# The output projection of an encoder layer on one core: x fetched in spaced pieces, evictions reordered, turned tiles spread

## The reference

```python
y = jax.nn.sigmoid(m_a) * ya + jax.nn.sigmoid(m_b) * yb
x = x + y @ w_out[i]
g = jax.nn.sigmoid(_rms(x, ple_norm[i]) @ w_ple_gate[i])
x = x + (p[i] @ w_ple[i]) * g
```

## Time and profile before

| | |
|---|---|
| median of 3 runs | 1808.4 us (1806.47 to 1808.62) |
| the profiled execution's own time | 1807.8 us |
| its span, from the first to the last instruction | 1806.1 us |
| TensorE busy | 1767.6 us, 98% of the span |
| VectorE busy | 1282.9 us, 71% |
| ScalarE busy | 865.1 us, 48% |
| DMA, mean over the span | 131 GB/s |

### The profile page before, as it was taken

The page is one execution under the profiler, slowest core; times in us unless marked ns, Lnnn a source line. Parts: engine busy times, 40 slices in busy tenths (PEclk is TensorE's granted clock), DMA queues, the critical chain, the costliest instruction groups (busy, mean ns, idle before and its releaser), DMA issues.

```text
span 1806.1 us, 23828 instructions
## 1 busy us (share of the span) xinstructions
PE 1767.6 (98%) x9241; PEld 1517.4 (84%) x9241; DVE 1282.9 (71%) x1546; ACT 865.1 (48%) x1169; POOL 196.9 (11%) x203
## 2 busy tenths in 40 slices
PE   6999999999999999999999999999999989899998
PEld 5899999888888888888888888888888768788887
DVE  6977777777687878787887878784555688864333
ACT  7444444434375757474747565654222434434221
POOL 4000000000040404040303131310000000000000
PEclk9999999999999999999999999999999999999999
DMA  7344444575723332333332333344555466432332
GB/s 225 90 140 118 116 138 144 195 253 176 201 82 110 87 108 81 109 86 111 87 109 83 103 88 106 92 134 134 164 148 154 141 234 216 145 129 92 118 117 82
DMA packets 289286, 236.81 MB, mean 131 GB/s; under 512 B 9994, under 2 KB 234281, under 8 KB 288673
## 3 DMA queue, kind: packets, MB, share of 16 engines
q1 hardware_dynamic: 286128, 225.49, 41.6%
q0 software_dynamic: 3056, 9.96, 1.7%
HBM read 215.00 MB, written 20.41 MB: 130 GB/s over the span
## 4 chain that ended last, share of the span: by engine, by line
PE 90%; DVE 5%; issue 2%; DMA 2%; ACT 1%; SPq 0%; DVEq 0%; ACTq 0%
PE mm_ps L2037 13%; PE mm_ps L2039 13%; PE mm_ps L2038 13%; PE ax_ps L2024 2%; PE ax_ps L2026 2%; PE ax_ps L2025 2%; PE ax_ps L2038 2%; PE ax_ps L2037 2%; PE ax_ps L2039 2%; PE mm_ps L2263 2%; PE mm_ps L2262 2%; PE mm_ps L2261 2%; PE mm_ps L2026 2%; PE mm_ps L2024 2%; PE mm_ps L2025 2%
## 5 line engine op out<-in xcount | busy, mean ns | idle before, releaser
L364 DVE TENSOR_TENSOR w_lo<-w_raw,w_hi 128x1024 fp32r<-128x1024 f32 x188 | 236.0, 1257 | 251.7 <-ACT w_hi L355 251.6
L2037 PE MATMUL mm_ps<-act_hl,w_hi 128*128 128x512 f32 x960 | 383.1, 399 | 0.0
L355 ACT ACTIVATE w_hi<-w_raw 128x1024 fp32r<-128x1024 f32 x188 | 198.5, 1056 | 375.7 <-PE mm_ps L2039 157.5
L2039 PE MATMUL mm_ps<-act_hl,w_lo 128*128 128x512 f32 x960 | 375.0, 391 | 0.0
L2038 PE MATMUL mm_ps<-act_hl,w_hi 128*128 128x512 f32 x960 | 374.6, 390 | 0.0
L2039 PEld LDWEIGHTS mm_ps<-act_hl,w_lo 128*128 128x128 f32 x960 | 180.2, 188 | 38.7
L2038 PEld LDWEIGHTS mm_ps<-act_hl,w_hi 128*128 128x128 f32 x960 | 180.5, 188 | 36.1
L2037 PEld LDWEIGHTS mm_ps<-act_hl,w_hi 128*128 128x128 f32 x960 | 180.5, 188 | 36.0
L1046 ACT ACTIVATE q_hi<-q_raw 128x1024 fp32r<-128x1024 f32 x84 | 87.6, 1057 | 141.7 <-DVE q_raw L1408 81.3
L1399 DVE TENSOR_TENSOR q_lo<-q_raw,q_hi 128x1024 fp32r<-128x1024 f32 x84 | 101.8, 1224 | 52.6 <-ACT q_hi L1046 52.1
L921 POOL TENSOR_TENSOR key<-key,low_h 128x512 f32<-128x512 f32 x16 | 16.8, 1052 | 804.6 <-ACT key L1153 804.6
(11 more groups left out here) (372 smaller groups left out, 4194.8 us busy)
## 6 DMA issues: line engine op xcount, KB each, us to landing
w_raw<-in_w_in SPq DMA_DIRECT2D x120, 512.0 KB, 3.8
q_raw<-in_w_in SPq DMA_DIRECT2D x56, 512.0 KB, 5.9
r_in<-in_w_in SPq DMA_DIRECT2D x56, 512.0 KB, 4.6
w_raw<-in_w_out SPq DMA_DIRECT2D x36, 512.0 KB, 4.8
w_raw<-in_w_ple_gate SPq DMA_DIRECT2D x32, 512.0 KB, 3.8
...
```

The source lines that it names most:

```text
L355: nc.scalar.activation(w_hi[:, s, :], w_raw[:, r, :], ACT.Copy).then_inc(hi_done, 1)
L364: nc.vector.tensor_tensor(w_lo[:, s, :], w_raw[:, r, :], w_hi[:, s, :].bitcast(F32), ALU.subtract).then_inc(lo_done, 1)
L2037: MM(bank, wh, m_hi[:, k0 + k, :], start=start and k == 0, stop=False)
L2039: mm = MM(bank, wl, m_hi[:, k0 + k, :], start=False, stop=stop and k == kn - 1)
```

## The change

- The column `norm_c` is no longer fetched by SP at step 9 of group 0, but by POOL, far ahead, right after its last work on the heads.
- The four pieces of x for a group are no longer issued at one go. In group 0 piece t waits in addition for TensorE to be done with step 3 + 2t, in group 1 with step 2t, the first of these behind eviction 2 of group 0 (before: eviction 2 too, which then stood at step 16 of group 0).
- Evictions get an order for each group (`O_ORDER`) and new places (`O_AT`, `O_AFTER`): in group 0 eviction 1 goes from step 14 to 22, 4 to 7 from 18, 22, 24, 26 to 23 to 26, and evictions 2, 3 and 8 follow 9 and 10 into steps 1 to 5 of group 1. In group 1 the places stay. `ev(g, n, t)` turns an eviction into the count that a wait needs.
- The `sy_lo` of group 0 go from steps 4, 6, 9, 12 to 5, 7, 11, 15, and the last `y_lo` from step 4 to 6.
- The six turned tiles go from after steps 17 to 22 of group 1 to after steps 17, 18, 21, 22, 25, 26; tile 5's low part goes behind the first `w_lo` of the gate projection. `token_squares` goes from steps 4 to 11 to steps 8 to 15.

The diff, without most of its unchanged lines:

```diff
@@ -482,6 +482,15 @@
         SY_AT = {2: 1, 3: 2, 6: 3, 5: 4}
+        O_ORDER = ((0, 1, 4, 5, 6, 7, 2, 3, 8, 9, 10), tuple(range(11)))
+        O_AT = ({14: 0, 22: 1, 23: 4, 24: 5, 25: 6, 26: 7}, {13: 0, 14: 1, 16: 2, 17: 3, 18: 4, 22: 5, 24: 6, 26: 7, 27: 8})
+        O_AFTER = {1: 2, 2: 3, 3: 8, 4: 9, 5: 10}
+        TURN_AT = {17: 0, 18: 1, 21: 2, 22: 3, 25: 4, 26: 5}
+        def ev(g, n, t=1):
+            return 22 * g + 2 * O_ORDER[g].index(n) + t + 1
@@ -823,8 +832,6 @@
                         bring_gates(sp, KT - 1)
-                    if g == 0 and j == 9:
-                        sp.dma_start(pn_c[:, :], pn_v).then_inc(pn_in, 16)
@@ -951,6 +958,7 @@
+            pool.dma_start(pn_c[:, :], pn_v).then_inc(pn_in, 16)
             pool.wait_ge(za_stored, 16 * (H - 1))
@@ -973,11 +981,13 @@
             for t in range(NT):
+                pool.wait_ge(unit_done, U_OUT + 4 + 2 * t)
                 pool.dma_start(x2a[:, t, :], x_v[:, t, 0:1024]).then_inc(xo_in[t], 16)
             pool.wait_ge(sy_lo_done, 4)
-            pool.wait_ge(o_ev, 6)
+            pool.wait_ge(o_ev, ev(0, 2))
             for t in range(NT):
                 k = 4 * (t % 2)
+                pool.wait_ge(unit_done, U_OUT + OUT_STEPS + 1 + 2 * t)
                 pool.dma_start(act_x[:, t // 2, k:k + 4, S // 2:S],
@@ -1275,7 +1285,7 @@
                 else:
-                    act.wait_ge(o_ev, 22 * g - 2)
+                    act.wait_ge(o_ev, ev(g - 1, 9))
                 for t in range(2):
@@ -1304,10 +1314,10 @@
                         o_copy(g)
-                    if g == 1 and 4 <= j < 12:
-                        token_squares(0, j - 4)
-                    if g == 1 and 20 <= j < 20 + TURN_EARLY:
-                        h2_hi_tile(j - 20)
+                    if g == 1 and 8 <= j < 16:
+                        token_squares(0, j - 8)
+                    if g == 1 and j - 2 in TURN_AT:
+                        h2_hi_tile(TURN_AT[j - 2])
@@ -1315,6 +1325,8 @@
                 split_hi(act, Units(U_PLE), i)
+                if i == 0:
+                    h2_hi_tile(TURN_EARLY - 1)
             for c in range(4):
@@ -1836,7 +1848,7 @@
-                first, done = U_OUT + OUT_STEPS * g, 22 * g
+                first = U_OUT + OUT_STEPS * g
                 brought = 16 * (g + 1)
@@ -1848,38 +1860,41 @@
                         dve.wait_ge(o_p1, 2 * g + t + 1)
-                        dve.wait_ge(o_ev, done + 1 + t)
+                        dve.wait_ge(o_ev, ev(g, 0, t))
                         o, x, y = x11, x11, u
...
                     elif n == 3:
+                        if g == 0:
+                            dve.wait_ge(o_ev, ev(g, 6, t))
                         o, x, y = x12, x12, pieces(o_bank(2, t))
...
                         dve.wait_ge(unit_done, first + 16)
-                        dve.wait_ge(o_ev, done + 3 + t)
+                        dve.wait_ge(o_ev, ev(g, 1, t))
                         o, x, y = u, pieces(o_bank(3, t)), u
                     elif n == 5:
-                        dve.wait_ge(o_ev, done + 9 + t)
+                        dve.wait_ge(o_ev, ev(g, 4, t))
                         o, x, y = x12, x12, u
...
                         dve.wait_ge(unit_done, first + 22)
-                        dve.wait_ge(o_ev, done + 11 + t)
+                        dve.wait_ge(o_ev, ev(g, 5, t))
                         o, x, y = x12, x12, pieces(o_bank(6, t))
...
                         dve.wait_ge(unit_done, first + 24)
-                        dve.wait_ge(o_ev, done + 11 + t)
+                        dve.wait_ge(o_ev, ev(g, 5, t))
                         o, x, y = u, pieces(o_bank(5, t)), u
                     elif n == 8:
-                        dve.wait_ge(o_ev, done + 15 + t)
+                        dve.wait_ge(o_ev, ev(g, 7, t))
+                        dve.wait_ge(o_ev, ev(g, 2, t))
                         o, x, y = x22, x22, u
                     elif n == 9:
-                        dve.wait_ge(o_ev, done + 15 + t)
+                        dve.wait_ge(o_ev, ev(g, 7, t))
                         o, x, y = x21, x21, u
...
                         dve.wait_ge(unit_done, first + 28)
-                        dve.wait_ge(o_ev, done + 19 + t)
+                        dve.wait_ge(o_ev, ev(g, 9, t))
                         o, x, y = x21, x21, pieces(o_bank(4, t))
@@ -1894,19 +1909,18 @@
                         y_sums(7)
-                    if g == 0 and j in (4, 6, 9, 12):
-                        sy_lo({4: 1, 6: 2, 9: 4, 12: 3}[j], {4: 1, 6: 2, 9: 3, 12: 4}[j])
-                    if g == 0 and j == 4:
+                    if g == 0 and j in (5, 7, 11, 15):
+                        sy_lo({5: 1, 7: 2, 11: 4, 15: 3}[j], {5: 1, 7: 2, 11: 3, 15: 4}[j])
+                    if g == 0 and j == 6:
                         y_lo(KT - 1)
-                    for n, at in enumerate((13, 14, 16, 17, 18, 22, 24, 26, 27)):
-                        if j == at:
-                            o_evict(g, n)
-                    if g and j in (1, 2):
-                        o_evict(g - 1, 8 + j)
+                    if j in O_AT[g]:
+                        o_evict(g, O_AT[g][j])
+                    if g and j in O_AFTER:
+                        o_evict(g - 1, O_AFTER[j])
                     if j + 2 in ROW_SUMS:
                         o_weight_sum(g, j + 2)
-                    if g == 1 and 21 <= j < 21 + TURN_EARLY:
-                        h2_lo_tile(j - 21)
+                    if g == 1 and j - 2 in TURN_AT:
+                        h2_lo_tile(TURN_AT[j - 2])
@@ -1920,6 +1934,7 @@
             split_lo(dve, Units(U_PLE), 0)
+            h2_lo_tile(TURN_EARLY - 1)
             o_evict(1, 9)
@@ -2267,7 +2282,7 @@
                 if k < 2:
-                    pe.wait_ge(o_ev, 30)
+                    pe.wait_ge(o_ev, ev(1, 3))
                 elif k < TURN_EARLY:
@@ -2290,11 +2305,11 @@
                     elif kp == 0 and u < 4:
-                        pe.wait_ge(o_ev, 22 * (g - 1) + (16, 14, 8, 22)[u])
+                        pe.wait_ge(o_ev, ev(g - 1, (7, 6, 3, 10)[u]))
                     if kp == 0 and u == 5:
...
                     if kp == 0 and u in (4, 6):
-                        pe.wait_ge(o_ev, 22 * g + {6: 2, 4: 10}[u])
+                        pe.wait_ge(o_ev, ev(g, {6: 0, 4: 4}[u]))
                     if kp == 0 and g == 0 and u in SY_AT:
@@ -2315,8 +2330,8 @@
                     mm.then_inc(unit_done, 1)
-                    if g == 1 and 17 <= j < 17 + TURN_EARLY:
-                        turn_x2(j - 17)
+                    if g == 1 and j in TURN_AT:
+                        turn_x2(TURN_AT[j])
@@ -2346,11 +2361,11 @@
                             elif t < 2:
-                                pe.wait_ge(o_ev, 38)
+                                pe.wait_ge(o_ev, ev(1, 7))
                         for w in range(2):
...
                             if c == 0 and t == 0:
-                                pe.wait_ge(h2_lo, max(k + 1, TURN_EARLY))
+                                pe.wait_ge(h2_lo, k + 1)
                             yield w, h2_tok(0, k, t), h2_tok(1, k, t), acc(t), k == 0, k == KT - 1
```

## The result

The changed kernel takes 1796.66 us (median of 4 runs, 1796.17 to 1796.85); the kernel before, beside it, 1808.46. The ratio is 0.9937, with a 95% interval of 0.992 to 0.9954: 11.8 us gained, 0.6%, and clear of the noise. The forecast was 1794.3 us, the range 1790.5 to 1799.9. The profiled execution took 1796.85 us, its span is 1795.1.

The account below looks back on a forecast made before the run. TensorE ends the kernel, so only its waits count: the stretch loses 21.6 us before, 2.5 + 2.7 + 2.1 + 0.85 = 8.1 after. Gain 13.5: 1807.8 - 13.5 = 1794.3 us, range 1790.5 to 1799.9 with rivals 1 and 2 mostly in it.

Parts of the forecast that it names:

- Steps 5 to 8: Group 0, new `sy_lo` and `y_lo` order: new waits of 2.5 us where there was about 1.1; alone a loss.
- The pieces of x, group 0: Load for the sum of step 11 goes ahead of the pieces, lands by 1448.6, no wait; step 13's load also in time.
- the stop at step 10: Group 0 before the change: TensorE's wait of 2.5 us and its 1.7 us at the slow clock, forecast to go.
- slack 1.5 us: Group 0, load for the sum of step 13: lands at 1454.8, VectorE comes to it at 1456.3.
- my second rival: Pieces of x still push a needed load back, stall of 2.5 us and fall of 1.7 return: 1799.8 us, chance 0.11.
- The end of group 0: Group 0 from about step 20 on: small waits of 2.7 us, in place of 3.4 and 3.0 at the slow clock.
- what is left there is what group 1 shows: 6.0 us: Group 0, step 20: 6.0 us from the end of step 19's `w_lo` to the sum of step 22, as in group 1.
- again behind four pieces of x: Group 0, step 20, before the change: a load took 7.36 us from 1477.43 because four pieces of x were ahead.
- the stop at step 20: Group 0 before the change: TensorE's wait of 3.4 us and 3.0 us at the slow clock, forecast to become small waits.
- The end of group 1: Turned tiles: old waits there go, new waits of 1.0 us at step 21 and 1.1 at step 25, together 2.1.
- The clock: New waits at most 1.75 us; slow-clock loss between 0 and 1.7 us, taken as 0.85.
- The column, `token_squares`, evictions 2, 3, 8, 9, 10 in group 1: Column through POOL at about 1182 us, `token_squares` within ScalarE's slack, evictions in steps 1 to 5 of group 1: cost 0.

## Why the prediction was right, point by point

**Its frame held.** Only the stretch changed, the gain is a gain in TensorE's waits and clock, and every wait left is released by a `w_lo`.

**Steps 5 to 8: right.** Predicted 2.5 us, in waits of 0.6 at step 6, 0.1 at step 7 and 1.75 at step 8. Measured: 0.61, 0.17 and 1.82 us of loss at these steps. (What the prediction calls a wait is the lateness of a step, so the loss is its measure; the idle time in the rows is 0.3 us less.) (All of steps 0 to 9 lose 2.90, but 0.3 of that, at step 4, is in the kernel before too.) That this part alone is a loss is shown by the run with the order put back: 1.25 us less there, 1.8 us in all.

**The pieces of x, group 0: half right.** That the load for the sum of step 11 now stands ahead of them, and lands in time (5.6 us was the bound), is right; it is shown by the kernel with the `sy_lo` order alone, in which the stop at step 10 is gone. The spacing had no part in it. "With the 8.50 us of the earlier trace rows it lands at 1454.8 … slack 1.5 us" is the term that was mis-sized. The load took 10.64 us and came 0.5 us too late: 0.96 us of loss where I had 0. This was my second rival in small, without its fall of the clock.

**The end of group 0: the size was off, and the cause half of the truth.** Predicted 2.7 us, measured 4.07. The step that failed is "what is left there is what group 1 shows: 6.0 us". In group 0 it is 7.3 us; the load of the chain takes 6.80 us there and 5.79 in group 1. SP issues the `r_mid` load 1.6 us ahead of the three in group 0 (1474.37, 1475.99) and 2.3 us ahead in group 1 (1554.99, 1557.33), so it has less of a start. The versions in the table of the `sy_lo` section bear this out but for one: with 2.7 us of start the load takes 5.0 us and steps 20 and 21 lose nothing. What shortens the start is VectorE's lateness, and in the changed kernel the `sy_lo` order brings it: with that order back, the end of group 0 loses 2.26 us and not 4.07. So the order that the prediction charged with 2.5 us at steps 5 to 8 costs again at steps 20 and 21, and this path, from VectorE's lateness through SP's issue to the load, is what the prediction left out. And the sentence "again behind four pieces of x" named only one of two causes of the stop at step 20. The runs with the evictions back show the other: the pairs of evictions in steps 16 to 18 delay the `w_lo` of step 19, on which SP's loads wait, and so steps 20 and 21 lose 3.5 us even with no x under way. In the changed kernel, the evictions are worth 2.2 us, and the x behind them 1.2 to 1.4. The prediction counted from the end of that `w_lo` and took from group 1 that TensorE starts step 19 2.8 us behind it. In the changed kernel it is 2.85 us, with the evictions back 0.6. So the start of its count was right, but only thanks to the moved evictions, which it didn't name as the reason.

**The end of group 1: right.** Predicted 1.0 and 1.1 us of wait at steps 21 and 25, 2.1 in all; measured 1.00 and 0.65 us of idle time, 1.31 and 0.96 of loss, and 2.54 for the whole end. The run with the tiles alone shows that this is the largest part, 7.0 of 21.6 us.

**The clock: 0 where I had 0.85.** No wait of up to 1.53 us was followed by a fall. The Trainium skill (TensorE: Matmul & The Clock Gate, "HAM oscillation — how this bites in real kernels") would have made this term 0, and the measurement agrees with it here; in the kernel before it doesn't, where the clock fell behind a wait of 2.54 us.

**The column, `token_squares`, evictions 2, 3, 8, 9, 10 in group 1: right,** at 0. The column was tried by itself, and steps 0 to 16 of group 1 lose nothing. `token_squares` was not tried by itself.

**The sum.** 2.5 + 2.7 + 2.1 + 0.85 = 8.1 was predicted, 2.9 + 1.0 + 4.1 + 2.5 + 0 = 10.5 measured: 2.4 us more, which is what lies between 1794.3 and 1796.7. The two errors that matter, 1.0 and 1.4 us, are loads that took longer than the rows that I took for them; the clock gave 0.85 back, so the time is nearer than its terms. The gate projection starts 165.4 us after the first step, not 163.

**What the parts are worth together.** Alone, in the profiled stretch, tiles, evictions, spacing and `sy_lo` order give 7.0, 3.7, 3.6 and -0.3 us: 14.0, where all of them give 11.1. Three of these kernels (all but the tiles) also pay 1.2 to 1.6 us for the longer slow clock at tile 2, which the full change doesn't have; without it the single gains would add up to still more, about 18. Evictions and spacing cure the same stop at step 20, the `sy_lo` order and the spacing the one at step 10. (The evictions alone also take the x of group 1 away from step 20, as said there.) Once the evictions and the order are in, the spacing is worth nothing.
